# Moving the start addresses of the split weights and of the moving tiles in SBUF by three gaps

## What is computed

```python
def _conv_ffn(xn, w_up, conv_w, conv_b, w_down):
    up = xn @ w_up                      # 2048 -> 2 * 5632
    u, g = up[..., :D_FF], up[..., D_FF:]
    g = causal_conv_width_3(g, conv_w) + conv_b
    return (jax.nn.silu(g) * u) @ w_down  # 5632 -> 2048
```

## The kernel before

| tile | starts at | modulo 256 | streams or is loaded on L639 |
|---|---|---|---|
| `wr`, `w1` | 32896 | 128 | loaded, except in `tokens_out` |
| `raw` | 65664 | 128 | neither |
| `ys` | 107456 | 192 | streams |
| `xs`, `xm` | 185280 | 192 | streams, loaded in `tokens_out` |

## Time and profile before

### The profile page before, as it was taken

The page is one execution under the profiler, slowest core; times in us unless marked ns, Lnnn a source line. Parts: engine busy times, 40 slices in busy tenths (PEclk is TensorE's granted clock), DMA queues, the critical chain, the costliest instruction groups (busy, mean ns, idle before and its releaser), DMA issues.

```text
span 2833.5 us, 44014 instructions
## 1 busy us (share of the span) xinstructions
PE 2766.6 (98%) x15284; PEld 2388.8 (84%) x15284; DVE 1981.3 (70%) x2609; ACT 1189.0 (42%) x1517; POOL 5.7 (0%) x12
## 2 busy tenths in 40 slices
PE   6899999999999999999999999999999999999999
PEld 4787888888878888888888888888888888888888
DVE  6555477676767777756777666688777775677765
ACT  1102454444444444444444543355444444444443
POOL 0000000000000000000000000000000000000000
PEclk9999999999999999999999999999999999999999
DMA  9886655544545666666666566654466666666664
GB/s 295 291 265 196 208 188 181 175 139 144 160 129 170 179 187 192 183 192 189 183 188 191 183 193 190 181 163 126 152 182 185 190 184 193 187 187 185 191 199 144
DMA packets 704736, 527.14 MB, mean 186 GB/s; under 512 B 31693, under 2 KB 694031, under 8 KB 704399
## 3 DMA queue, kind: packets, MB, share of 16 engines
q1 hardware_dynamic: 701728, 523.67, 61.1%
q10 hardware_dynamic: 2927, 2.39, 0.3%
HBM read 523.87 MB, written 2.10 MB: 186 GB/s over the span
## 4 chain that ended last, share of the span: by engine, by line
PE 89%; DVE 5%; issue 2%; ACT 2%; DMA 1%; ACTq 0%; DVEq 0%; SPq 0%
PE acc L639 76%; PE acc L719 2%; PE acc L707 2%; PE acc L908 2%; PE turned L719 1%; DVE wr L1646 1%; PE sums L719 1%; DVE pro_ada L1721 1%; DMA aring<-in_w_ada 1%; PE sums L647 1%; PE mixed L829 1%; PE sums L1023 1%; PE mixed L1028 0%; ACT wr L1205 0%; ACTq L1236 0%
## 5 line engine op out<-in xcount | busy, mean ns | idle before, releaser
L639 PE MATMUL acc<-xs,wr 128*128 128x512 f32 (+1 forms) x7680 | 1365.2, 339 | 1.1 <-DVE wr L1646 1.1
L639 PEld LDWEIGHTS acc<-xs,wr 128*128 128x128 f32 x7680 | 1176.8, 188 | 177.2 <-issue 7.2
L1646 DVE TENSOR_TENSOR wr<-raw,wr 128x1024 fp32r<-128x1024 f32 x832 | 1001.8, 1222 | 363.6 <-ACT wr L1205 351.7
L1205 ACT ACTIVATE wr<-raw 128x1024 fp32r<-128x1024 f32 x832 | 869.7, 1057 | 818.6 <-PE acc L639 812.1
L639 PE MATMUL acc<-ys,wr 128*128 128x512 f32 (+1 forms) x4352 | 769.5, 338 | 6.7 <-DVE ys L1680 6.5
L639 PEld LDWEIGHTS acc<-ys,wr 128*128 128x128 f32 x4352 | 668.4, 188 | 103.1 <-DVE ys L1680 6.4
L639 PE MATMUL acc<-wr,xs 128*128 128x512 f32 (+1 forms) x1024 | 190.1, 344 | 0.0
L639 PEld LDWEIGHTS acc<-wr,xs 128*128 128x128 f32 x1024 | 158.2, 188 | 27.1 <-issue 4.3
L1539 ACT ACTIVATE ffn_cv<-ffn_cv 128x256 f32<-128x256 f32 x88 | 36.8, 419 | 245.8 <-DVE ffn_cv L2220 245.8
L1657 DVE TENSOR_REDUCE ffn_ug<-acc 128x512 f32<-128x1024 f32 x88 | 107.8, 1225 | 42.5 <-PE acc L639 42.5
L1721 DVE SCALAR_TENSOR_TENSOR pro_ada<-aring,small,pro_ada 128x512 f32<-128x512 f32 (+1 forms) x112 | 92.5, 826 | 30.1 <-DMA aring<-in_w_ada 23.5
(11 more groups left out here) (306 smaller groups left out, 1530.4 us busy)
## 6 DMA issues: line engine op xcount, KB each, us to landing
raw<-in_ffn_w_up SPq DMA_DIRECT2D x704, 256.0 KB
raw<-in_ffn_w_down SPq DMA_DIRECT2D x160, 512.0 KB
raw<-in_a_w_qkv SPq DMA_DIRECT2D x96, 512.0 KB
raw<-in_b_w_kv SPq DMA_DIRECT2D x64, 512.0 KB
aring<-in_w_ada SPq DMA_DIRECT2D x96, 256.0 KB, 6.8
w<-in_w_in SPq DMA_DIRECT2D x48, 512.0 KB
raw<-in_w_ada SPq DMA_DIRECT2D x32, 512.0 KB, 5.7
raw<-in_w_out SPq DMA_DIRECT2D x32, 512.0 KB
```

Of the source, the lines that this page charges most:

```text
L639: mm = pe.matmul(*ops, start=first and ops is wide, stop=last and ops is wide)
L1205: f(wr[:, s, :, 0:256], raw[:, s, :].rearrange("p (k n) -> p k n", k=UK), ACT.Copy)\
L1646: tt(wr[:, s, :, 256:512], raw[:, s, :].rearrange("p (k n) -> p k n", k=UK), wr[:, s, :, 0:256], ALU.subtract).then_inc(T.unit_split[s].se ...
```

## The change

Three calls of a new function `begin_at` take a small unused tensor where needed, so that the next tile begins at a wanted address modulo 256.

```diff
+WEIGHTS_STEP, MOVING_STEP = 160, 64
...
+        def begin_at(name, step):
+
+            skip = (step - nc.sbuf_base) % 256
+            if skip:
+                sb(name, [skip // 4])
+
         h = sb("h", [KT, TOK])
+        begin_at("weights_gap", WEIGHTS_STEP)
         wr_at = nc.sbuf_base
         wr = sb("wr", [RING, UK, 512], F32R)
...
         ARENA = 32 * 1024
+        begin_at("slab_gap", MOVING_STEP)
         slab = ctx.enter_context(nc.sbuf_tensor("slab", [P, YS + ARENA], mybir.dt.uint8))
         base = nc.sbuf_base - (YS + ARENA)
+        begin_at("stream_gap", MOVING_STEP)
         xs = sb("xs", [KT, 2 * TOK], F32R)
```

## The result

The changed kernel takes 2819.36 us in the median of 5 runs (2817.65 to 2820.61), against 2834.24 us before. The ratio is 0.9944 with a 95% interval of 0.993 to 0.9959, so it is 14.9 us faster. The profiled execution has a span of 2817.6 us, 15.9 us less than before.

What follows compares the result with a forecast made beforehand. TensorE was taken as the bound, through what each matmul costs in its stream. Gains of 23.5 us (usual pairs) and 4.0 us (tokens_out), together 27.5, took 2835.3 to 2807.8 us, median 2807; range 2749 to 2858 us.

Steps and rivals of the forecast that it cites:

- case A: Split-product pairs: partial relief of 0.9 to 13 ns each, 2749 to 2828 us, likeliest 2807; chance 0.42.
- excess of 25.9 ns: Usual pairs: 349.3 ns less the 323.4 ns floor, read as weight loads and stream getting in each other's way.
- 3.9 ns between the two roles: Pairs before: 349.3 ns in usual roles, 353.2 in tokens_out, taken as a hint that start addresses matter.
- Rival C: Split-product pairs: starts don't matter, all pairs keep their time, 2829 to 2840 us; chance 0.22.
- the pair's: Split-product pairs go to 345.4 ns in both roles: 23.5 us gained in usual roles, 4.0 us in tokens_out.
- Case D: Split-product pairs: the new distance is worse, 2857 us at 353.2 ns a pair, 2881 at twice that step; chance 0.23.
- upper bound of 353.2 ns: Usual pairs: the one worse arrangement in the trace, from tokens_out, would lose 23.5 us.
- Case B: Split-product pairs: nearly all the excess goes, 85 to 171 us gained, 2663 to 2749 us; chance 0.13.
- floor of 323.4 ns: A pair's least time: 215.6 ns for the wide matmul, from first-block plain float32 matmuls, plus 107.8 for the short one.
- plain matmuls: Float32 matmuls of the first block: already at their floor of 215.6 ns, sixteen still in 3.45 us, change taken as 0.
- splitting steps: Splitting on VectorE (1222 ns) and ScalarE (1057 ns): times should stay, covered by TensorE's stream, change taken as 0.
- waits of TensorE: Sign to check in the new profile: TensorE's waits should be those of before, longest sum 7.7 us.

Runs made afterwards that it cites:

- moving_only: Changed kernel with the split weights back at 128, ys and xs still at 64 (distance 192, in tokens_out 64); 2852.25 us, ratio 1.0059 to the kernel before.
- same_distances: Changed kernel with the split weights at 128, ys at 32 (distance 160) and xs at 160 (distance 32); 2821.63 us, ratio 0.9948 to the kernel before.
- old_distances: Changed kernel with the split weights at 160, ys at 224 (distance 64) and xs at 96 (distance 192); 2847.33 us, ratio 1.004 to the kernel before.

## Why the prediction was right, and where it was off

**The range and case A held; the direction was mostly luck.** 2819 us lies in 2749 to 2858 and in case A. The gain was 14.9 us where 27 were forecast. The mechanism behind the gain, a price that depends on the distance, was forecast with a reason. That 160 would be on the good side was not: the prediction called its reason weak. It was that an excess of 25.9 ns leaves more room below than 353.2 shows above. The room wasn't there: no start tried took a pair under 346.8 ns. Of the seven other distances in steps of 32, two are better than the 64 of before and five are worse.

**The hint in the trace was a true one.** The prediction took the 3.9 ns between the two roles as a sign that starts matter, and chose the distance of the starts as the cause. moving_only shows it: with the distances changed over, the roles change their prices over. Rival C is refuted for matmuls at this rate: eight distances gave 346.8 to 352.8 ns a pair. The Trainium skill, "SBUF — State Buffer", section "SBUF: two separate sides", has it that TensorE's port waits on nobody, and gives weight loads a second, independent read port. As the prediction read it, that leaves no room for the distance of two starts to matter. These measurements disagree with that.

**The term that was mis-sized is the pair's.** I took one step of 3.9 ns downwards, to 345.4 ns for both roles. Distance 160 gives 346.8 ns, so the step is 2.5 ns and the term 15.0 us in place of 23.5. The 3.9 ns were the step from 64 to 192, and nothing tied the step from 64 to 160 to it. For `tokens_out` I took 345.4 ns as well, a gain of 7.8 ns a pair. Its new distance is 96, which costs 350.7 ns, so its term is 1.3 us in place of 4.0. For the same reason the two roles did not come closer together, as I had written: each distance has its own price.

**The price of the other cases.** Case D was a real danger: of the eight distances at multiples of 32, three cost 3 to 3.5 ns a pair more than before (0, 192, 224) and two cost 1 to 1.5 ns more (96, 128). Moving the streamed tiles alone, one half of this change, makes the kernel 0.59% slower. The prediction's upper bound of 353.2 ns was right: no distance in steps of 32 was above it. My argument for D, that 160 is no multiple of 64, is refuted by same_distances and old_distances. Case B's floor of 323.4 ns was far from everything measured: no start tried gave less than 346.8 ns, and at distance 160 a load that stands still, or lasts half as long, still gives 346.5. So little seems to be left for the loads' addresses to give. That is argued from one distance, and not every start was tried.

**The inference on the excess was wrong in its larger part.** The prediction read the whole 25.9 ns as loads and stream in each other's way. Measured at distance 160: 16.6 ns (346.5 - 329.9) go when the stream stands still and stay when the load does. Another 6.5 ns (329.9 - 323.4) stay with both still. The load's moving address accounts for the rest, 0.3 ns. At the 64 of before and at 192 the pair takes 2.8 and 6.3 ns more than 346.5. That this is loads against stream is likely, since the distance of the two decides it, but no kernel had a load that stands still at those distances.

The 16.6 ns do not come from the other engines. The trace of the changed kernel shows it, by the single starts of the matmuls that stream `xs` or `ys`. With VectorE and ScalarE both idle, the next start came 228.9 ns after that of a wide matmul (175 of them) and 118.0 ns after that of a short one (202), 346.8 ns together. With no DMA packet under way it was 229.4 and 117.4 ns (908 and 1016), again 346.8. With VectorE, ScalarE and DMA all busy throughout it was 230.1 and 117.1 ns (828 and 1098), 347.2 together. That is 0.4 ns between quiet and busy. Why a moving stream costs 16.6 ns is open.

**The terms taken as nothing were nothing.** The plain matmuls, the splitting steps and the waits of TensorE stayed close to what the rows of before show, with the list of waits of the changed kernel beside the earlier trace rows:

```profile
PE acc L649 <- DVE ys L1690: 6.6, 3, 3.4
PE sums L657 <- ACT sq L1255: 6.5, 1, 6.5
PE acc L717 <- DVE xm L1749: 6.2, 5, 1.7
...
PE acc L649 <- DVE wr L1656: 1.7, 8, 0.2
```

One count in the margin for the splitting steps was wrong. The prediction gave the busiest stretch 176 units of VectorE; that number is the size of a sample in the earlier trace rows. One unit feeds 8 pairs (6528 pairs and 832 units in all, a few of them not full), so the 704 pairs need 88 units. Steps that are 10% longer would have added 88 x 0.12 = 11 us and made VectorE 83% busy, not 87%. The term stays 0 either way.

## What to carry to other kernels

Where TensorE streams float32r at one column a step, the distance between the starts of the streamed and the loaded tile, modulo 256 bytes, was worth up to 6 ns in a pair of 350 in this kernel. Look at products whose roles are exchanged in the same trace: they show two distances for nothing. Move a tile only with a measurement beside it, since five of the eight distances in steps of 32 were worse than the one the kernel had by accident.

## What the runs showed of the hardware that was not expected

- The price of a pair is not smooth in the distance: 32, 144, 160 and 208 are good (346.8 to 347.3 ns), 0, 192 and 224 are bad (352.2 to 353.2 ns), and 176, only 16 bytes past 160, takes 350.0. The 144 is good in the usual roles alone, and 208 was measured in `tokens_out` alone.
- Streamed tiles that begin 8 bytes off a multiple of 16 took 353.3 ns between two distances that take 346.8.
- A stream that reads one column over and over takes 329.9 ns a pair, 16.9 ns less than one that moves. Halving the loads from 128 to 64 columns, 188 to 134 ns each, changed the pair by 0.3 ns, which is the error of the reading.
- At distance 160 a pair took 346.8 ns with VectorE and ScalarE idle and 347.2 with both and DMA busy.
